# A two-layer hybrid encoder: high parts of the feed-forward weights by casting transfer instead of by ScalarE

## The reference

```
proj = h @ w_in[l]                       # four head groups: windowed attention, short
...                                      # convolution, Fourier mixing, dense attention
h = layer_norm(DN_ALPHA * h + mix @ w_out[l], ln1_g[l], ln1_b[l])
ffn = jnp.square(jax.nn.relu(h @ w1[l])) @ w2[l]      # 1024 -> 4096 -> 1024
h = layer_norm(DN_ALPHA * h + ffn, ln2_g[l], ln2_b[l])
```

## Time and profile before

| | |
|---|---|
| time, median of 3 runs | 1066.15 us (1065.83 to 1067.42) |
| span of the profiled execution | 1066.1 us |
| TensorE busy | 1052.3 us, 99% |
| VectorE busy | 776.2 us, 73% |
| ScalarE busy | 536.6 us, 50% |
| GpSimd busy | 99.0 us, 9% |
| moved by DMA | 105.47 MB, mean 99 GB/s |

### The profile page before, as it was taken

The page is one execution under the profiler, slowest core; times in us unless marked ns, Lnnn a source line. Parts: engine busy times, 40 slices in busy tenths (PEclk is TensorE's granted clock), DMA queues, the critical chain, the costliest instruction groups (busy, mean ns, idle before and its releaser), DMA issues.

```text
span 1066.1 us, 15182 instructions
## 1 busy us (share of the span) xinstructions
PE 1052.3 (99%) x5249; PEld 892.5 (84%) x5249; DVE 776.2 (73%) x1075; ACT 536.6 (50%) x809; POOL 99.0 (9%) x90
## 2 busy tenths in 40 slices
PE   7999999999999999999999999999999999999997
PEld 6888889998888888888888888899888888888885
DVE  7845886878757758758787568777884784785687
ACT  3433666565355355355634247655643642652654
POOL 5200232100000000000002003221000000000003
PEclk9999999999999999999999999999999999999999
DMA  7432023031521420430333410311234134125122
GB/s 289 159 118 79 2 60 120 6 122 40 195 81 39 175 101 23 174 119 38 121 134 147 158 40 21 109 52 48 80 120 156 40 101 175 39 82 194 40 80 79
DMA packets 17378, 105.47 MB, mean 99 GB/s; under 512 B 2016, under 2 KB 2704, under 8 KB 5792
## 3 DMA queue, kind: packets, MB, share of 16 engines
q1 hardware_dynamic: 15984, 98.70, 25.6%
q0 software_dynamic: 1184, 5.86, 1.7%
q10 hardware_dynamic: 144, 0.07, 0.0%
HBM read 101.49 MB, written 2.10 MB: 97 GB/s over the span
## 4 chain that ended last, share of the span: by engine, by line
PE 98%; DMA 1%; DVE 0%; POOL 0%; ACT 0%; DVEq 0%; issue 0%; SPq 0%; POOLq 0%; ACTq 0%
PE bank L457 19%; PE bank L458 18%; PE bank L459 18%; PE bank L798 9%; PE bank L797 9%; PE bank L796 9%; PE bank L739 4%; PE bank L725 2%; PE bank L466 1%; PE bank L636 1%; PE bank L637 1%; PE bank L526 1%; PE bank L533 1%; PE bank L540 1%; DMA w_raw<-in_weights 1%; PE bank L649 1%
## 5 line engine op out<-in xcount | busy, mean ns | idle before, releaser
L457 PE MATMUL bank<-h_hi,w_hi 128*128 128x512 f32 (+1 forms) x688 | 257.8, 375 | 0.0
L458 PE MATMUL bank<-h_lo,w_hi 128*128 128x512 f32 (+1 forms) x688 | 257.5, 374 | 0.0
L459 PE MATMUL bank<-h_hi,w_lo 128*128 128x512 f32 (+1 forms) x688 | 257.4, 374 | 0.0
L796 PE MATMUL bank<-w_hi,hid_hi 128*128 128x512 f32 x448 | 174.4, 389 | 0.0
L798 PE MATMUL bank<-w_hi,hid_lo 128*128 128x512 f32 x448 | 174.3, 389 | 0.0
L797 PE MATMUL bank<-w_lo,hid_hi 128*128 128x512 f32 x448 | 174.3, 389 | 0.0
L1233 DVE TENSOR_TENSOR w_lo<-w_raw,w_hi 128x2048 fp32r<-128x2048 f32 x62 | 141.9, 2288 | 39.2 <-ACT w_hi L912 32.7
L912 ACT CAST w_hi<-w_raw 128x2048 fp32r<-128x2048 f32 x56 | 107.1, 1913 | 85.6 <-PE bank L798 61.5
L457 PEld LDWEIGHTS bank<-h_hi,w_hi 128*128 128x128 f32 x688 | 129.5, 188 | 23.1
L458 PEld LDWEIGHTS bank<-h_lo,w_hi 128*128 128x128 f32 x688 | 129.5, 188 | 23.1
L459 PEld LDWEIGHTS bank<-h_hi,w_lo 128*128 128x128 f32 x688 | 129.5, 188 | 23.1
(11 more groups left out here) (180 smaller groups left out, 1648.1 us busy)
## 6 DMA issues: line engine op xcount, KB each, us to landing
w_raw<-in_weights SPq DMA_DIRECT2D x63, 1024.0 KB, 4.8
w_third<-in_weights SPq DMA_DIRECT2D x23, 1024.0 KB, 4.7
rows<-in_rows POOLq DMA_DIRECT2D x4, 1024.0 KB, 4.8
w_raw<-in_weights SPq DMA_DIRECT2D x4, 512.0 KB, 9.4
out_h<-x SPq DMA_DIRECT2D x8, 256.0 KB, 2.0
x<-in_x SPq DMA_DIRECT2D x3, 512.0 KB, 10.8
dft<-in_dft SPq DMA_DIRECT2D x2, 512.0 KB, 6.5
qk_gain<-in_qk_gain POOLq DMA_DIRECT2D x3, 192.0 KB, 3.4
```

The costliest lines, as they stand in the source:

```text
L457: pe.matmul(dst, s_hi, m_hi, start=first, stop=False)
L458: pe.matmul(dst, s_hi, m_lo, start=False, stop=False)
L459: return pe.matmul(dst, s_lo, m_hi, start=False, stop=last)
L796: pe.matmul(bank[dst + t][:], s_hi, m_hi, start=start, stop=False, skip_group_check=goes_on)
```

## The change

In the feed-forward chunks, ScalarE no longer copies the seven plain blocks. GpSimd issues for each a transfer of the same block from HBM straight into the slot of `w_hi`, of type fp32r, so that the transfer casts. SyncE still loads the raw block, since VectorE takes the low part from it. VectorE now waits for the cast transfer (`high_landed` of the slot) and for the raw load. GpSimd's loop over layers is written out. A cast transfer is issued when the slot is released, by the same counts as before.

```diff
+CAST_OF_SLOT = ((B11, B21, CHUNK_OPERANDS + W0), (CHUNK_OPERANDS + W1,), (W2,), (W3, B22))
...
             def split_in_chunk(l, c, i):
...
-                if i in (T1, T2, T3, T4):
-                    act.wait_ge(sems["w_sum"], l * (4 * CHUNKS) + c * 4 + ((T1, T2, T3, T4).index(i) + 1))
-                elif i in (B22, B21):
-                    act.wait_ge(third_landed, l * (48 * CHUNKS) + c * 48 + (16 if i == B22 else 32))
...
+                act.wait_ge(sems["w_sum"], l * (4 * CHUNKS) + c * 4 + ((T1, T2, T3, T4).index(i) + 1))
                 act.wait_ge(sems["products"], l * PER_LAYER["products"] + c * CHUNK_G + (MLP_G0 + RELEASED[i]))
                 act.copy(w_hi[:, SLOT[i], :], raw_of(i)).then_inc(sems["w_hi"], 1)
...
-                    split_in_chunk(l, c, W2)
...
-                        if i == 0:
-                            split_in_chunk(l, c, W3)
...
-                        if i == 0:
-                            split_in_chunk(l, c, B11)
-                    for i in (B22, T3, B21, T4):
+                    for i in (T3, T4):
                         split_in_chunk(l, c, i)
-                    if not last:
-                        for i in range(2):
-                            split_of_next_chunk(l, c, i)
...
             def split_in_chunk(l, c, i):
-                dve.wait_ge(sems["w_hi"], operand(l, c, i + 1))
...
+                    dve.wait_ge(high_landed[slot], l * (16 * casts_of_layer(slot)) + c * per_chunk + 16 * (CAST_OF_SLOT[slot].index(i) + 1))
+                    if i in (B22, B21, CHUNK_OPERANDS + W0):
+                        dve.wait_ge(third_landed, l * (48 * CHUNKS) + c * 48 + 16 * ((B22, B21, CHUNK_OPERANDS + W0).index(i) + 1))
...
-            with pool.Fori(0, DEPTH) as l:
+            for l in range(DEPTH):
...
+                def cast_high(c, i):
+                    block_of = {W2: 2, W3: 3, B11: 4, B22: 6, B21: 7, CHUNK_OPERANDS + W0: 8, CHUNK_OPERANDS + W1: 9}[i]
+                    released = NEXT_RELEASED[i - CHUNK_OPERANDS] if i >= CHUNK_OPERANDS else RELEASED[i]
+                    slot = SLOT[i % CHUNK_OPERANDS]
+                    pool.wait_ge(sems["products"], l * PER_LAYER["products"] + c * CHUNK_G + (MLP_G0 + released))
+                    pool.dma_start(w_hi[:, slot, :], w_in[l * BLOCKS + MLP0 + c * CHUNK_BLOCKS + block_of]).then_inc(high_landed[slot], 16)
+
+                for c in range(CHUNKS):
+                    for i in (W2, W3, B11, B22, B21):
+                        cast_high(c, i)
+                    if c < CHUNKS - 1:
+                        for i in range(2):
+                            cast_high(c, CHUNK_OPERANDS + i)
```

More of the change, by code:

```diff
@@ L93 @@
 PER_LAYER = dict(
-    w_hi=MLP0 + CHUNKS * CHUNK_OPERANDS, w_lo=MLP0 + CHUNKS * CHUNK_OPERANDS, w_sum=4 * CHUNKS, gained_hi=3, gained_lo=3, w_hi_part=2 * (PARTS - 1), w_lo_part=2 * (PARTS - 1), products=MLP_G0 + CHUNKS * CHUNK_G,
+    w_hi=MLP0 + 2 + 4 * CHUNKS, w_lo=MLP0 + CHUNKS * CHUNK_OPERANDS, w_sum=4 * CHUNKS, gained_hi=3, gained_lo=3, w_hi_part=2 * (PARTS - 1), w_lo_part=2 * (PARTS - 1), products=MLP_G0 + CHUNKS * CHUNK_G,
     turned=4 * TOK, h_hi=4 * TOK, h_lo=4 * TOK,
@@ L106, with casts_of_layer @@
 )
+CAST_OF_SLOT = ((B11, B21, CHUNK_OPERANDS + W0), (CHUNK_OPERANDS + W1,), (W2,), (W3, B22))
+def casts_of_layer(slot):
+    return CHUNKS * len(CAST_OF_SLOT[slot]) - (CAST_OF_SLOT[slot][-1] >= CHUNK_OPERANDS)
 def head_of(j, kv):
@@ L307, in build @@
         third_landed = sem("third_landed")
+        high_landed = [sem(f"high_landed{s}") for s in range(RING)]
         ident_landed = sem("ident_landed")
@@ L901, in split_in_chunk @@
             def split_in_chunk(l, c, i):
-                if i in (T1, T2, T3, T4):
-                    act.wait_ge(sems["w_sum"], l * (4 * CHUNKS) + c * 4 + ((T1, T2, T3, T4).index(i) + 1))
-                elif i in (B22, B21):
-                    act.wait_ge(third_landed, l * (48 * CHUNKS) + c * 48 + (16 if i == B22 else 32))
[L907 to L910, removed]
+                act.wait_ge(sems["w_sum"], l * (4 * CHUNKS) + c * 4 + ((T1, T2, T3, T4).index(i) + 1))
                 act.wait_ge(sems["products"], l * PER_LAYER["products"] + c * CHUNK_G + (MLP_G0 + RELEASED[i]))
                 act.copy(w_hi[:, SLOT[i], :], raw_of(i)).then_inc(sems["w_hi"], 1)
-            def split_of_next_chunk(l, c, i):
-                if i == 0:
[L917 to L921, removed]
             act.wait_ge(const_set, 2)
@@ L1231, in split_in_chunk @@
             def split_in_chunk(l, c, i):
-                dve.wait_ge(sems["w_hi"], operand(l, c, i + 1))
+                if i in (T1, T2, T3, T4):
+                    dve.wait_ge(sems["w_hi"], l * PER_LAYER["w_hi"] + c * 4 + (MLP0 + 2 + (T1, T2, T3, T4).index(i) + 1))
+                else:
+                    slot = SLOT[i % CHUNK_OPERANDS]
+                    per_chunk = 16 * len(CAST_OF_SLOT[slot])
+                    dve.wait_ge(high_landed[slot], l * (16 * casts_of_layer(slot)) + c * per_chunk + 16 * (CAST_OF_SLOT[slot].index(i) + 1))
+                    if i in (B22, B21, CHUNK_OPERANDS + W0):
+                        dve.wait_ge(third_landed, l * (48 * CHUNKS) + c * 48 + 16 * ((B22, B21, CHUNK_OPERANDS + W0).index(i) + 1))
+                    elif i in (W3, CHUNK_OPERANDS + W1):
+                        dve.wait_ge(w_landed[1], l * (16 * LANDED[1]) + c * 48 + 16 * (MLP0 // RAW + (2 if i == W3 else 4)))
+                    else:
+                        dve.wait_ge(w_landed[0], l * (16 * LANDED[0]) + c * 32 + 16 * (MLP0 // RAW + (2 if i == W2 else 3)))
                 dve.tensor_tensor(w_lo[:, SLOT[i % CHUNK_OPERANDS], :], raw_of(i),
@@ L1855, in _ @@
                 load_params(l + 1)
+                def cast_high(c, i):
+                    block_of = {W2: 2, W3: 3, B11: 4, B22: 6, B21: 7, CHUNK_OPERANDS + W0: 8, CHUNK_OPERANDS + W1: 9}[i]
+                    released = NEXT_RELEASED[i - CHUNK_OPERANDS] if i >= CHUNK_OPERANDS else RELEASED[i]
+                    slot = SLOT[i % CHUNK_OPERANDS]
+                    pool.wait_ge(sems["products"], l * PER_LAYER["products"] + c * CHUNK_G + (MLP_G0 + released))
[6 more added lines that the diff above has]
+                            cast_high(c, CHUNK_OPERANDS + i)
                 wait(pool, l, "hidden_lo", 12 * CHUNKS)
                 load_rows(2 * l + 2)
-                with pool.If(l < DEPTH - 1):
+                if l < DEPTH - 1:
                     layer_norm_rstd(2 * l + 2)
```

## The result

The changed kernel takes 1071.18 us (median of 4 runs, 1070.63 to 1071.5) against 1065.99 us of the kernel before on the same chip (1065.34 to 1067.42). The ratio is 1.0046 with a 95% interval of 1.003 to 1.0062. It is slower by 5 us, clear of the scatter. That lies inside the range of the prediction, but it is not the forecast case, which was no change.

A forecast was written before the change was run, and what follows sets the result against it. TensorE was taken as the bound, busy 1052.3 of 1066.1 us, with ScalarE's copies beside the path. Gain 0 and cost 0 on the 1066.1 us span gave 1066.2 us, no change; range 1065 to 1076.

The forecast's parts named there:

- the forecast case: Whole kernel: no wait of TensorE appears and the time stays at 1066.2 us, 1065.2 to 1067.5; chance 0.70.
- D: Feed-forward chunks: time from a slot's release to the landing of its cast transfer, taken as 5 to 6 us.
- The rival of a slow cast: TensorE waits for low parts of the next W0, then B21, from 8.4 us landing time; 1069.8 to 1099; chance 0.25.
- the growth of D beside an instruction of VectorE: GpSimd's descriptor writing might wait for a VectorE TENSOR_TENSOR, adding up to 2.3 us: 7.1, still below 8.4.
- B22 and B21: Tight weight blocks in a chunk: B22's first loss at about 9 us landing time, B21 with 11.9 us to spare.
- The chain that I walked through: Low B22, load of B21, T4's difference, low B21: ends at 353.15, needed at 355.19, 2.0 us to spare.
- VectorE needs 2.28 us for the low part. So D may be 371.5 - 360.8 - 2.3 = 8.4 us: Next chunk's W0, 6 times: the cast may take 8.4 us; at 5.5 the low part ends 2.9 us early.
- The wait of VectorE of about 2 us: Expected sign: VectorE's low part of the next W0 waits for a DMA for about 2 us.
- a lone landing over 8.4 us: Sign of a wrong prediction: a lone cast lands that late, and TensorE waits on low parts, six at chunk ends first.
- my rivals: Slow cast, 0.25; TensorE faster, about 1062 us, 0.05; bits moved unrounded with zero low parts, 1066.2, inside the forecast.
- no wait appears: Forecast's case: TensorE's waits list nothing new and the time does not change; chance 0.70.
- Price of each: 0: What is added: 52 transfers of 1 MB, GpSimd's issue, VectorE's semaphore waits, the later load of `rows`; nothing on the path.

The follow-up runs named there:

- run 8: The changed kernel with the next chunk's W0 and W1 back on ScalarE, 40 casts staying: 1067.15 us, ratio 1.0008 to the kernel before.
- run 1: The changed kernel with the add of T3's second tile placed before the low part of the next W0 on VectorE: 1067.97 us, ratio 1.002.
- run 6: The changed kernel with that add before the low part of the next W0, plus an early drain of GpSimd before its last norms: 1066.73 us, ratio 1.0005.
- Run 2: The kernel before with GpSimd's layer loop written out and 52 more 9 KB GpSimd transfers into an unread buffer: 1067.98 us, ratio 1.0019.
- early drain: The changed kernel with one more GpSimd drain before its last norms, where it idles; VectorE's order as in the change: 1069.93 us, ratio 1.0038.

## Why the prediction was right and where it was wrong

**Right: TensorE is the bound, freed time on ScalarE gives nothing.** ScalarE lost 95.5 us (forecast 99.5) and the chunk copies that are left are 32:

```profile
L913 ACT CAST w_hi<-w_raw 128x2048 fp32r<-128x2048 f32 x32 | 61.3, 1915 | 97.0 <-PE bank L806 55.4 <-DVE w_raw L1247 41.6
```

The pace of the matmuls stayed at 222 to 50 us where no stall was.

**Right: D.** I took 5 to 6 us from GpSimd's plain transfer. The casts of the next W0, B22 and B21 land in 4.9 to 5.2 us, those of W3, issued right behind W2's, in 8.7 to 10.2. All 52 together, by the view of the casts' line:

```profile
L1857 POOL DMA_DIRECT2D w_hi<-in_weights x52: 527/528/568, 209.7 to 1027.2; - x52
...
DMA to landing us min/median/max: 4.9/5.1/10.2
```

The rival of a slow cast did not come: neither half the rate nor a third. Nor did the growth of D beside an instruction of VectorE: the cast of B21 was issued at 337.92, with a low part on VectorE from 337.94 to 340.22, and landed in 5.0 us; the next W1's at 365.12, inside the low part that began at 364.78, in 5.0 us too. One number under it was low: full DMA engines were put at 312 GB/s and moved 405. Whether a plain transfer of the same block would land sooner than a cast was not tried; GpSimd's plain transfers of `rows` took 4.8.

**Right: B22 and B21.** The chain that I walked through held its times, and run 8 has no wait of TensorE in a chunk with both of them cast.

**Wrong: the step "VectorE needs 2.28 us for the low part. So D may be 371.5 - 360.8 - 2.3 = 8.4 us".** It asked when TensorE needs the low part, and not who stands behind it on VectorE. Behind it stands the add of T3's second tile (the changed kernel's row at 366.99), and T4's second product needs its two banks to have been read. In the changed kernel that product was due at 367.16 + 0.23 = 367.39, 7.7 us after the issue of the cast. Take from that 2.2 us for the low part and 0.7 for the add, and D may be 4.8 us. It is 5.1 to the start of the low part: the add ends at 367.67, 0.3 us late. I had also taken the start of ScalarE's copy as the moment of the cast's issue, and GpSimd issued 0.26 us later after the release than ScalarE began. That is nearly all of the 0.3 us; no run takes it away by itself. With the weight load behind it and the slower first matmul that makes the 0.45 us at this place. Six of them are the 3.0 us of the trace, and 2.8 us between the changed kernel and run 1 (1.0046 and 1.002). The wait of VectorE of about 2 us was forecast, and it was the warning. The sign by which I would have known myself wrong, a lone landing over 8.4 us, never came, and TensorE waited all the same. None of my rivals held this case, to which I had left no chance: 0.70 stood on "no wait appears".

**Wrong: "Price of each: 0" for the 52 transfers.** Their issue and traffic cost nothing that run 6 can tell (0.5 us, with an interval of -0.4 to 1.5). What I had no term for is GpSimd's closing drain: 52 x 0.082 = 4.3 us longer, 2.6 of it covered by the last output transfer, 1.6 left. Run 2 measures it as 2.0 us with an interval of 1.0 to 3.0, run 1 as 2.1. (The barrier of the changed kernel shows 1.2, not 1.6, since its own last output transfer took 2.1 us in that execution and not 1.7.)

**The sum.** 3.0 + 1.6 = 4.6 us against 4.9 measured (interval 3.2 to 6.6). The table of two by two, each against the kernel before: neither mended 1.0046, add first 1.002, early drain 1.0038, both 1.0005. Taken from the last, the drain alone costs 1.6 us and the stalls alone 3.5; with its 0.5 they make 5.6 against the 4.9 of the change, the same within the intervals. The time fell in the range only because the range was widened for a slow cast, and the cause that widened it did not happen. That is luck: the forecast's own case was 1065.2 to 1067.5, and it was missed by both terms that I had put at nothing.

## What to carry to other kernels

When an engine's wait gets longer, read its stream on to the next instruction whose result the bounding engine waits for, and price the deadline of that one. A low part whose transfer could take 8.4 us stood ahead of an add that left it 4.8. Where a wait is moved onto a transfer, put the urgent short work ahead of it; here one swapped line gave back 3 us. When GpSimd issues many transfers, read its closing drain at the end of the trace, and if it comes last, drain once where GpSimd is idle; here that gave back 0.9 to 1.9 us.

## What the runs showed of the hardware that I had not expected

GpSimd's drain takes 0.082 us for each transfer that GpSimd issued since the last drain, independent of size and of casting (14, 26, 54 and 66 transfers: 1.23, 2.21, 4.50, 5.48 us). With 118 it took 4.66 us, as for 56, so by this rate about 62 had been settled earlier; what settles them was not tried. An early drain of 5.45 us took the whole of it. A cast from float32 to fp32r in a transfer of 1 MB lands, alone, within 0.3 us of a plain one of GpSimd (5.1 against 4.8 us, medians), and the cast of W3 beside SyncE's loads ran at 405 GB/s. After the same event GpSimd's issue began 0.26 us later than ScalarE's copy (0.69 and 0.43 us after the start of the matmul that releases the slot).
